# VectorE turns the normed heads of q and k, attention starts one unit later, and the loops of three engines are written out

## The reference, cut to what matters

```
q, k, v = jnp.split(h @ w_in, 3, axis=-1)
q = rms_norm(split_heads(q, SB_HEADS, SB_HEAD_DIM), q_gain).astype(jnp.float32)
k = rms_norm(split_heads(k, SB_HEADS, SB_HEAD_DIM), k_gain).astype(jnp.float32)
q = q * (SB_HEAD_DIM ** -0.5)
z = jnp.einsum('bhqd,bhkd->bhqk', qb, k)
```

## Time and profile before

| | |
|---|---|
| time, median of 3 runs | 1225.83 us (1225.28 to 1226.48) |
| profiled execution: its time, its span | 1226.86 us, 1223.9 us |
| granted TensorE clock, mean | 0.999 |
| TensorE matmuls busy | 1217.5 us, 99% of the span |
| VectorE / ScalarE / GpSimd busy | 818.2 / 588.2 / 73.1 us |
| one attention group (24 units) on TensorE | 75.16 us |

### The profile page before, as it was taken

One profiled execution on the slowest core, in us unless ns is written; L12 is line 12 of the kernel. 1 busy time (PEld: TensorE's weight loads), 2 busy tenths in 40 slices (PEclk: granted clock), 3 DMA queues, 4 the chain that ended last, 5 costly groups with the idle time before them and its releaser, 6 DMA issues.

```text
span 1223.9 us, 17011 instructions
## 1 busy us (share of the span) xinstructions
PE 1217.5 (99%) x5524; PEld 1011.1 (83%) x5524; DVE 818.2 (67%) x1039; ACT 588.2 (48%) x727; POOL 73.1 (6%) x126
## 2 busy tenths in 40 slices
PE   9999999999999999999999999999999999999998
PEld 7888888888888888888888888888888888888886
DVE  5667576675779865776776677577665666655555
ACT  6555465554645534444443444444444444444443
POOL 0411102011000300000000000000000000002000
PEclk9999999999999999999999999999999999999999
DMA  7655465555555666666666666666565656474674
GB/s 267 209 184 161 151 189 157 185 154 160 174 165 173 208 190 203 191 190 186 205 190 186 205 189 187 189 205 187 173 216 164 221 164 225 154 229 152 192 230 131
DMA packets 120004, 229.32 MB, mean 187 GB/s; under 512 B 7538, under 2 KB 8868, under 8 KB 119972
## 3 DMA queue, kind: packets, MB, share of 16 engines
q1 hardware_dynamic: 119940, 228.90, 60.5%
q10 hardware_dynamic: 32, 0.01, 0.0%
HBM read 226.78 MB, written 2.10 MB: 187 GB/s over the span
## 4 chain that ended last, share of the span: by engine, by line
PE 66%; DMA 1%; DVE 0%; issue 0%; ACT 0%; ACTq 0%; SPq 0%; DVEq 0%
PE acc L1047 66%; DMA raw<-in_ple_w_gate 1%; DVE w_lo L702 0%; PE T L1080 0%; DVE stage L1011 0%; DVE x L1014 0%; DVE side L903 0%; ACT w_hi L443 0%; ACT stage L677 0%; SPq L264 0%; ACTq L442 0%; ACTq L440 0%; ACTq L671 0%; ACTq L676 0%; ACTq L674 0%
## 5 line engine op out<-in xcount | busy, mean ns | idle before, releaser
L702 DVE TENSOR_TENSOR w_lo<-raw,w_hi 128x1024 fp32r<-128x1024 f32 (+1 forms) x445 | 524.2, 1185 | 293.3 <-ACT w_hi L443 289.6
L443 ACT ACTIVATE w_hi<-raw 128x1024 fp32r<-128x1024 f32 (+1 forms) x445 | 452.6, 1021 | 552.8 <-PE acc L1047 514.5
L1047 PE MATMUL acc<-w_hi,xT_hi 128*128 128x512 f32 x1204 | 472.8, 393 | 0.3
L1047 PE MATMUL acc<-w_hi,xT_lo 128*128 128x512 f32 x1204 | 469.6, 390 | 0.0
L1047 PE MATMUL acc<-w_lo,xT_hi 128*128 128x512 f32 x1204 | 469.2, 390 | 0.0
L1047 PEld LDWEIGHTS acc<-w_hi,xT_hi 128*128 128x128 f32 x1204 | 226.2, 188 | 48.0 <-issue 1.3
L1047 PEld LDWEIGHTS acc<-w_hi,xT_lo 128*128 128x128 f32 x1204 | 226.1, 188 | 47.5
L1047 PEld LDWEIGHTS acc<-w_lo,xT_hi 128*128 128x128 f32 x1204 | 226.3, 188 | 45.6
L1047 PE MATMUL acc<-w_hi,hT_hi 128*128 128x512 f32 x352 | 137.1, 390 | 0.0
L1047 PE MATMUL acc<-w_lo,hT_hi 128*128 128x512 f32 x352 | 137.1, 390 | 0.0
L1047 PE MATMUL acc<-w_hi,hT_lo 128*128 128x512 f32 x352 | 137.1, 390 | 0.0
(11 more groups left out here) (133 smaller groups left out, 626.1 us busy)
## 6 DMA issues: line engine op xcount, KB each, us to landing
raw<-in_sb_w_in SPq DMA_DIRECT2D x93, 512.0 KB, 3.7
raw<-in_ffn_w_gate SPq DMA_DIRECT2D x88, 512.0 KB, 3.7
raw<-in_ffn_w_up SPq DMA_DIRECT2D x88, 512.0 KB, 4.0
raw<-in_ffn_w_down SPq DMA_DIRECT2D x80, 512.0 KB, 4.7
raw<-in_sb_w_out SPq DMA_DIRECT2D x32, 512.0 KB, 3.8
raw<-in_ple_w_gate SPq DMA_DIRECT2D x20, 512.0 KB, 5.6
raw<-in_ple_w_gate SPq DMA_DIRECT2D x24, 256.0 KB, 3.3
raw<-in_ffn_w_down SPq DMA_DIRECT2D x16, 256.0 KB, 3.1
```

Source lines behind the costliest of these rows:

```text
L443: act.activation(w_parts[0][:, slot(u), 0:n, :], raw[:, slot(u), 0:n, :], ACT.Copy).then_inc(hi_ready, 1)
L702: dve.tensor_tensor(w_parts[1][:, slot(u), 0:n, :], raw[:, slot(u), 0:n, :], w_parts[0][:, slot(u), 0:n, :].bitcast(F32), ALU.subtract).th ...
L1047: last = pe.matmul(acc[pair][tb][:, :], parts[a][:, c, tb * P:(tb + 1) * P], w_parts[w][:, slot(u), i, :], start=(start and i == 0 and n = ...
```

## The change

The transposes of `normed` leave TensorE. `norm_heads` writes `normed` with one operation a block that takes `rstd` and GpSimd's `head_r`; VectorE then turns it with 16 transposes of 32x32 blocks (32 partitions by 256 elements each): q's into a new SBUF buffer `q_side` over six units (13 to 18), k's into `k_side`, which is the memory of `squares`, over three units (20 to 22). The hi parts are one ScalarE operation of 128x1024 each (q at u = 20, k at u = 0 of the next group), and the lo parts one on VectorE (q at u = 21, k at u = 1 of the next group). Attention on all engines comes one unit later within the groups (`A_FROM = 1`), and as before in stage B. GpSimd's `head_norm` has 6 operations in place of 11: the mean square is now two small operations of VectorE behind `sum_heads`, and the scale goes into the Newton step. The loops of ScalarE, VectorE and GpSimd are written out; TensorE's and SyncE's stay.

```diff
+    A_FROM = 1
+    Q_NORM, Q_TURN, Q_UNITS, Q_HI, Q_LO = 13, 13, 6, 20, 21
+    K_NORM, K_TURN, K_UNITS, K_HI, K_LO = 20, 20, 3, 0, 1
...
+            k_side = squares[:, :, :].rearrange("p t n -> p (t n)").rearrange("p (h s) -> p h s", h=HG)
...
             def sum_heads(n):
                 dve.wait_ge(squares_ready, n + 1)
-                dve.wait_ge(head_scale_ready, n)
+                dve.wait_ge(head_r_ready, n)
                 dve.reduce_sum(head_ssq[:, :], squares[:, :, :].rearrange("p t (h d) -> p (t h) d", d=HD),
                                AX_X).then_inc(head_ssq_ready, 1)
...
+                dve.wait_ge(head_ssq_ready, n + 1)
                 for tb in range(TB):
+                    part = slice(tb * HG, (tb + 1) * HG)
+                    dve.tensor_scalar(head_ms[:, part], head_ssq[:, part], rstd2[:, tb:tb + 1], 1.0 / HD,
+                                      ALU.mult, ALU.mult).then_inc(head_ms_ready, 1)
...
+            def norm_heads(n, pair, q_turned, k_turned):
+                dve.wait_ge(head_r_ready, n + 1)
+                dve.wait_ge(q_side_ready, q_turned)
+                dve.wait_ge(k_side_ready, k_turned)
+                for tb in range(TB):
+                    root = head_r[:, tb * HG:(tb + 1) * HG].unsqueeze(2).broadcast_to([P, HG, HD])
+                    dve.scalar_tensor_tensor(out=normed[:, tb, :].rearrange("p (h d) -> p h d", d=HD),
+                                             in0=acc[pair][tb][:, :].rearrange("p (h d) -> p h d", d=HD),
+                                             scalar=rstd[:, tb:tb + 1], in1=root,
+                                             op0=ALU.mult, op1=ALU.mult).then_inc(acc_free[pair][tb], 1)
...
+            def turn_k(g, i):
+
+                if i == 0:
+                    left(dve, 1, A_P1 + g + 1)
+                    dve.wait_ge(kT_ready, g)
+                    dve.wait_ge(head_ssq_ready, 2 * g + 2)
+                for a, b in QUADRANTS[i * QN * QN // K_UNITS:(i + 1) * QN * QN // K_UNITS]:
+                    last = turn_heads(k_side, a, b)
+                if i == K_UNITS - 1:
+                    last.then_inc(k_side_ready, 1)
...
+                        if u == K_LO:
+                            k_lo(g - 1)
                         if u == 1:
                             keep_v(g - 1)
-                        attend(u, g - 1, A_EVERY)
+                        attend(u - A_FROM, g - 1, A_EVERY)
...
-            with nc.Fori(1, GROUPS, engines=[mybir.EngineType.DVE], hint_back_edge=True) as g:
+            for g in range(1, GROUPS):
                 group(g)
...
             def scores(h, i, g):
-                left_T0 = (X_ROUNDS + 1) // 2 + 4 * (g + 1)
-                pe.wait_ge(T_free[0], left_T0)
+                pe.wait_ge(qT_ready, g + 1)
+                pe.wait_ge(kT_ready, g + 1)
...
-                        attend(u, g - 1, A_EVERY)
-                        for m in range(2):
-                            if u == (i + 1) * DU + 4 + 2 * m + (first and i == 0 and m == 0):
-                                left(pe, i, (A_P0 + 2 * g, A_P1 + g)[i] + 1)
-                                turn(0, normed, 2 * m, (X_ROUNDS + 1) // 2 + 4 * g + 2 * i + m)
+                        attend(u - A_FROM, g - 1, A_EVERY)
```

More of the change, by code:

```diff
@@ L424, in _ @@
             norm(1, heads_end)
-            with nc.Fori(0, XN, engines=[mybir.EngineType.Pool], hint_back_edge=True) as t:
+            for t in range(0, XN):
                 store_x(t, 0, D_P0 + t + 1)
@@ L578, in group @@
                     if not first:
+                        if u == K_HI:
+                            k_hi(g - 1)
                         if u == 1:
                             keep_v(g - 1, U0 - 1)
-                        attend(u, g - 1, A_EVERY)
-                    for part, (to, gain) in enumerate(((qT, QG), (kT, KG))):
+                        attend(u - A_FROM, g - 1, A_EVERY)
+                    for part in range(2):
                         end = (part + 1) * DU - 1
@@ L645, in _ @@
             gate_up(0, first=True)
-            with nc.Fori(1, FN, engines=[mybir.EngineType.Activation], hint_back_edge=True) as j:
+            for j in range(1, FN):
                 gate_up(j)
@@ L661, in _ @@
             down(0, first=True)
-            with nc.Fori(1, XN, engines=[mybir.EngineType.Activation], hint_back_edge=True) as n:
+            for n in range(1, XN):
                 down(n)
@@ new lines, in turn_heads, with turn_q @@
+            def turn_heads(to, a, b):
+                return dve.transpose(
+                    to[b * Q:(b + 1) * Q, :, :].rearrange("p h (t s) -> p t h s", t=TB)[:, :, :, a * Q:(a + 1) * Q],
+                    normed[a * Q:(a + 1) * Q, :, :].rearrange("p t (h d) -> p t h d", d=HD)[:, :, :, b * Q:(b + 1) * Q])
+            def turn_q(g, i):
+                if i == 0:
+                    left(dve, 0, A_P0 + 2 * g + 1)
+                    dve.wait_ge(qT_ready, g)
+                for a, b in QUADRANTS[i * QN * QN // Q_UNITS:(i + 1) * QN * QN // Q_UNITS]:
+                    last = turn_heads(q_side, a, b)
+                if i == Q_UNITS - 1:
+                    last.then_inc(q_side_ready, 1)
@@ L836, in group @@
                     if not first:
-                        mask_scores(u, g - 1, A_EVERY)
+                        mask_scores(u - A_FROM, g - 1, A_EVERY)
                     if first and u == DU + 2:
@@ L860, in group @@
                             sum_heads(2 * g + part)
[L861 to L867, removed]
+                        if u == (Q_NORM, K_NORM)[part]:
+                            norm_heads(2 * g + part, part, g + part, g)
+                    if Q_TURN <= u < Q_TURN + Q_UNITS:
+                        turn_q(g, u - Q_TURN)
+                    if u == Q_LO:
+                        dve.wait_ge(q_hi_ready, g + 1)
+                        dve.scalar_tensor_tensor(out=qT[1][:, :, :], in0=q_side[:, :, :], scalar=gains[:, QG:QG + 1],
+                                                 in1=qT[0][:, :, :].bitcast(F32), op0=ALU.mult,
+                                                 op1=ALU.subtract).then_inc(qT_ready, 1)
+                    if K_TURN <= u < K_TURN + K_UNITS:
+                        turn_k(g, u - K_TURN)
             dve.wait_ge(gains_turned, 1)
@@ L979, in _ @@
             gate_up(0, first=True)
-            with nc.Fori(1, FN, engines=[mybir.EngineType.DVE], hint_back_edge=True) as j:
+            for j in range(1, FN):
                 gate_up(j)
@@ L999, in _ @@
             down(0, first=True)
-            with nc.Fori(1, XN, engines=[mybir.EngineType.DVE], hint_back_edge=True) as n:
+            for n in range(1, XN):
                 down(n)
```

79 lines of the change are left out of this document (35 added, 44 removed).

## The result

| | before | after |
|---|---|---|
| time, median (lowest to highest, runs) | 1226.15 us (1225.28 to 1227.12, 4) | 1239.71 us (1238.57 to 1240.42, 4) |
| ratio, 95% interval | | 1.0106 [1.0091, 1.0121] |
| span of the profiled execution | 1223.9 us | 1236.8 us |
| granted TensorE clock, mean | 0.999 | 0.996 |

The changed kernel is 1.06% slower, 13.6 us. The prediction said 1224.6 us, with a range that ended at 1228.4.

The account below looks back on a forecast made before the run. TensorE's own program was taken to bound the kernel: 7.84 us of transposes leave it, 6.56 us of new waits for VectorE come, so -1.28 from 1225.83 gives about 1224.6 us. Range 1220.2 to 1228.4.

Parts of the forecast that it names:

- What costs nothing: Paragraph claiming no cost from GpSimd's kept operations, ScalarE's hi parts and the feeders' written-out loops.
- TensorE keeps its loops: On the written-out feeder loops: TensorE's own loops stay, counted as costing nothing.
- Behind stage B each stretch as long as before: Sign to look for after the groups: every stretch behind stage B keeps its length.
- I am wrong if TensorE's clock falls behind a wait: Sign of error; a fall to 1.2 GHz for 3 us after each forecast wait would add some 1.5 us four times.
- the forecast of -1.28: Whole kernel: -7.84 us removed from TensorE plus 6.56 us of new waits.
- The removal, -7.84: TensorE in the groups: 4 groups x 4 turns x 0.49 us leave its program.
- The queue of 23.24 us from 0.96: VectorE from k's sum of squares to `v_lo`, starting 0.96 after unit 15's end: `v_lo` there at 24.2, wanted at 22.44.
- GpSimd's 3.06 us: GpSimd's kept operations, started at about 2.5, end at 5.6, ahead of norm of k at 6.5: no cost.
- The wait, 1.76 at each boundary: TensorE at a group's first products waits 1.76 us for `v_lo`; between groups 2 and 3, and 3 and 4: 3.52.
- 1.97 forecast: Boundary between groups 1 and 2, without attention before it: TensorE waits 1.97 us for `v_lo`.
- 1.07 forecast: Into stage B, scores first: TensorE waits 1.07 us for kT_lo, and the scores then cover `v_lo`.
- The rival "slower": Products of unit 0: longer VectorE queue through late head_r or kT_hi, decisive from 0.95 us; 1230.6 us at 1.5; chance 0.18.

Follow-up runs that it names:

- after_pad: Changed kernel with 74 pairs of satisfied waits added to TensorE's program in the first group: 1227.96 us, 1.0015 against the kernel before.
- Experiments 1 to 4: Satisfied waits added to TensorE's program: in the changed kernel 1227.96 us (first group) and 1236.56 (stage D); in the kernel before 1235.38, 1227.23 and 1226.45.
- experiment 5: Loops of ScalarE, VectorE and GpSimd put back in the changed kernel, 1241.40 us; written out in the kernel before, 1225.84 us.
- before_pad: Kernel before with 182 pairs of satisfied waits in TensorE's first group, loop exits 15 and 7 instructions ahead of the boundary: 1235.38 us.
- pad_late: Changed kernel with 74 pairs of satisfied waits of TensorE in stage D's first projection: 1236.56 us.
- feeders_loop: Changed kernel with the loops of ScalarE, VectorE and GpSimd put back, TensorE's program untouched: 1241.40 us.
- k_three: Changed kernel with 74 pairs of satisfied TensorE waits in the first group, and only three of k's 16 transposes a group kept (computation incomplete): 1220.01 us, 0.995.
- before_30: Kernel before with 167 pairs of satisfied waits in TensorE's first group, loop exits 30 and 22 instructions ahead of the boundary: 1227.23 us.

## Why the prediction was wrong

**The step that failed** is in "What costs nothing": "TensorE keeps its loops". It keeps them, but its program became 74 instructions shorter, which moved each loop's exit against the fetch boundaries, and I counted only the time of what left. Hence also "Behind stage B each stretch as long as before": false from stage E's start on by 4.4 us (13.0 - 8.6), and at stage B by the 4.2 us by which the changed kernel's first product there (312.01) is later than after_pad's (307.82), with 1.9 us of slow clock behind it. These two make 10.5 of the 12.9 us. The section of the Trainium skill cited in that paragraph ("Runtime: NRT & Kernel Launch", "Instruction fetch mechanics") warns of taken branches, and I applied it to the feeders' loops alone, where it made no difference. Experiments 1 to 4 show that the place in the program makes the stops; experiment 5 rules the feeders' loops out.

**"I am wrong if TensorE's clock falls behind a wait".** It does, but not where I put it: not behind the forecast waits, only in the stops, which are 2.5 to 5.1 us of idle time in the four traces that have them at either place (after, before_pad, pad_late, feeders_loop).

**Right in kind, mis-sized: the groups.** Without the stops the forecast of -1.28 meets +2.6 us at the start of stage B (307.82 against 305.20), so the sign was wrong too. Term by term:

- *The removal, -7.84.* k_three gives 0.42 us a turn: -6.8. My 0.49 came from one pair of windows 5.44 and 5.93 us long; a difference of 0.07 was beyond them, and it counted 16 times.
- *The queue of 23.24 us from 0.96.* The trace of the changed kernel, VectorE from the sum of k's squares:

```profile
207.94 1.22 DVE L747 TENSOR_REDUCE head_ssq<-squares 128x8 f32<-128x1024 f32 x1
209.26 0.36 DVE L753 TENSOR_SCALAR head_ms<-head_ssq,rstd 128x4 f32<-128x4 f32 x2
...
214.10 1.41 DVE L762 SCALAR_TENSOR_TENSOR normed<-acc,rstd,head_r 128x512 f32<-128x512 f32 x2 [0.38 <-POOL head_r L384]
...
226.52 3.50 DVE L704 TENSOR_TENSOR w_lo<-raw,w_hi 128x1024 fp32r<-128x1024 f32 x3
229.93 1.28 DVE L796 SCALAR_TENSOR_TENSOR kT_lo<-squares,gains,kT_hi 128x1024 fp32r<-128x1024 f32 x1
231.13 1.41 DVE L804 SCALAR_TENSOR_TENSOR v_lo<-acc,rstd,v_hi 128x512 fp32r<-128x512 f32 x2
```

  Unit 15 ends at 207.06. The sum starts 0.88 later (0.96 forecast); norm of k starts at 7.04 (6.5 forecast), 0.38 of it waiting for GpSimd's head_r, which I had called hidden and had named as a sign of being wrong; TensorE goes on at 231.93, 24.87 after unit 15 against 24.2. Transposes at 436 ns, large lo parts of 1.28: as forecast. So a queue 0.67 longer, over half of it the wait for head_r. The term behind it is GpSimd's 3.06 us. Here its kept operations take 4.35, from 209.71 to 214.06: two that were 0.20 long before take 0.52 and, as this row has it, 1.10. Why they do is not shown.

```profile
212.68 1.10 POOL L382 TENSOR_SCALAR newton<-newton 128x8 f32<-128x8 f32 x1
```

- *The wait, 1.76 at each boundary.* The distances at 227.80 and 231.93 are 0.97 and 1.26 us over the usual 0.23: 2.2 in all. I saw one wait where there are two: a queue that is late for `v_lo` is late for the `lo` ahead of it as well. The sum would be the same, had the queue been right. And the first boundary, with a wait at unit 22 too, loses 2.9 (1.97 forecast), stage B 1.6 (1.07 forecast).
- Together: -6.8 + 2.9 + 2.3 + 2.2 + 1.6 = +2.2 of the 2.6; matmuls that start 0.1 us slower behind each wait may be the rest, which I have not shown.

**The rival "slower"** had the place and the mechanism of the groups right and was given 0.18; its threshold was a queue 0.95 longer, and it was 0.67. With the stops taken out the change stands at 1.0015, within 0.2%, which is what the forecast called likeliest; but it is a small loss and not a small gain, so only the width of that range makes it fit. That no stop is in the kernel before is luck of its layout: its exits happen to lie far from the boundaries.

## What to carry to other kernels

Before you cost an edit of an engine that loops, count how many instructions it adds to or takes from that engine's program: the loops' exits move against the 256-instruction packets, and an exit just ahead of a boundary cost TensorE 2.5 to 5.1 us of idle time here, at two places, with a slow clock behind it. Where a stretch that was not touched gets longer, look for a stop whose named releaser had long been done, or "issue", just behind a loop, and shift the program by some dozens of no-ops before believing any other story. And a queue that gives up its lead at the end of a stage is late for everything in it: move what nobody needs yet behind what the next stage waits for.

## What the runs showed of the hardware that I had not expected

- A satisfied wait on TensorE costs nothing that can be seen: 137 pairs, 1226.45 us against 1226.30.
- At stage E TensorE went on 3.5, 3.6, 3.5 and (feeders_loop) 3.1 us behind the loop's exit, whatever the distance to the boundary (some 7 or 22 instructions). At stage B it went on 4.7 to 6.0 us behind the first row after the loop in four traces, and in before_30 it did not stop at a boundary 2.3 us behind that row.
- Idle stretches of up to 1.27 us left the granted clock at 1.00. The stops, of 2.5 to 5.1 us of idle time, took it to 0.50, and matmuls started 0.43 us apart for 3 to 6 us behind them.
- The same GpSimd operation on 128x8 took 0.20 us in one kernel and 1.10 in the other (L370 before, L382 after).
